# Rows of 260 columns instead of 272 for the fp32r activations of a two-block transformer kernel

## What is computed

```
h = concat(meta_tokens, x)                                   # 272 tokens
proj = rmsnorm(h, norm1_w) @ w_in                            # q k v r glr pu
h = h + concat(o_gla, o_pool) @ w_out                        # mixed heads
h = h + square(relu(rmsnorm(h, norm2_w) @ mlp_w1)) @ mlp_w2  # inner width 8192
x = rmsnorm(h, final_norm_w)[16:]                            # 256 tokens
x = layer_norm(ALPHA * x + hybrid_mixer(x))                  # x @ w_in_2, @ w_out_2
x = layer_norm(ALPHA * x + (mem_attention(x @ w_q)) @ w_o)
x = layer_norm(ALPHA * x + (silu(x @ w_g) * (x @ w_u)) @ w_ffn_out)   # inner width 5632
```

## Time and profile before

| | before |
|---|---|
| median of 3 runs | 2639.5 us |
| lowest, highest | 2638.65, 2639.68 us |
| span of the profiled execution | 2636.7 us |
| mean granted TensorE clock in it | 0.999 |
| TensorE matmuls busy | 2614.3 us (99%), 17248 matmuls |
| VectorE busy | 1565.8 us (59%) |
| ScalarE busy | 1196.8 us (45%) |
| HBM | 177 GB/s over the span |

### The profile page before, as it was taken

How to read it: one execution, slowest core, us unless ns; L and a number is a source line. 1 busy time by engine, 2 the same in 40 slices (tenths; PEclk the granted TensorE clock), 3 DMA queues, 4 the chain that set the end, 5 groups by cost and what they waited for, 6 DMA issues and landing times.

```text
span 2636.7 us, 44070 instructions
## 1 busy us (share of the span) xinstructions
PE 2614.3 (99%) x17248; PEld 2386.1 (90%) x17248; DVE 1565.8 (59%) x2115; ACT 1196.8 (45%) x1608; POOL 27.1 (1%) x65
## 2 busy tenths in 40 slices
PE   9999999999999999999999999999999999999998
PEld 7999889889899899898998999988899988888886
DVE  5544755555555555565744556666866677666655
ACT  5543444444444344534444554444544444444442
POOL 1000000000000000000000000000000000000000
PEclk9999999999999999999999999999999999999999
DMA  7564455555555565564434455554477645777653
GB/s 250 176 179 120 172 178 184 185 190 186 195 178 190 191 188 183 170 222 129 146 128 159 151 186 186 181 209 161 138 198 191 181 169 195 189 191 191 191 183 120
DMA packets 467830, 468.81 MB, mean 178 GB/s; under 512 B 9294, under 2 KB 384190, under 8 KB 466910
## 3 DMA queue, kind: packets, MB, share of 16 engines
q1 hardware_dynamic: 465648, 459.31, 56.0%
q0 software_dynamic: 2064, 7.82, 0.8%
HBM read 464.93 MB, written 2.10 MB: 177 GB/s over the span
## 4 chain that ended last, share of the span: by engine, by line
PE 94%; DVE 3%; ACT 1%; DMA 1%; issue 0%; SPq 0%; DVEq 0%; ACTq 0%
PE ps L662 16%; PE ps L664 16%; PE ps L663 16%; PE ps L692 11%; PE ps L693 11%; PE ps L691 11%; PE ps L659 6%; PE ps L660 3%; DMA raw<-in_w_kv_mem 1%; DVE w_lo L2005 1%; PE ps L1069 1%; PE ps L1122 1%; PE ps L1128 1%; PE ps L752 0%; PE ps L1093 0%
## 5 line engine op out<-in xcount | busy, mean ns | idle before, releaser
L2005 DVE TENSOR_TENSOR w_lo<-raw,w_hi 128x1024 fp32r<-128x1024 f32 (+1 forms) x876 | 1053.2, 1210 | 843.7 <-ACT w_hi L1375 841.5
L1375 ACT ACTIVATE w_hi<-raw 128x1024 fp32r<-128x1024 f32 (+1 forms) x876 | 908.5, 1046 | 975.2 <-PE ps L664 475.7
L662 PE MATMUL ps<-xa,w_hi 128*128 128x256 f32 (+2 forms) x3328 | 951.1, 286 | 1.4 <-DVE w_lo L2005 1.4
L664 PE MATMUL ps<-xa,w_lo 128*128 128x256 f32 (+2 forms) x3328 | 941.0, 283 | 0.0
L663 PE MATMUL ps<-xa,w_hi 128*128 128x256 f32 (+2 forms) x3328 | 936.3, 281 | 0.0
L662 PEld LDWEIGHTS ps<-xa,w_hi 128*128 128x128 f32 x3328 | 627.6, 189 | 12.2 <-issue 9.5
L663 PEld LDWEIGHTS ps<-xa,w_hi 128*128 128x128 f32 x3328 | 629.3, 189 | 1.5 <-issue 0.5
L664 PEld LDWEIGHTS ps<-xa,w_lo 128*128 128x128 f32 x3328 | 627.8, 189 | 0.0
L659 PE MATMUL ps<-xa,w_hi 128*128 128x512 f32 x704 | 246.4, 394 | 0.0
L693 PE MATMUL ps<-w_hi,xh 128*128 128x512 f32 x512 | 201.2, 393 | 0.0
L692 PE MATMUL ps<-w_lo,xh 128*128 128x512 f32 x512 | 201.0, 392 | 0.0
(11 more groups left out here) (349 smaller groups left out, 2562.4 us busy)
## 6 DMA issues: line engine op xcount, KB each, us to landing
raw<-in_mlp_w SPq DMA_DIRECT2D x128, 1024.0 KB
raw<-in_w_in SPq DMA_DIRECT2D x106, 1024.0 KB
raw<-in_w_ffn_in SPq DMA_DIRECT2D x176, 512.0 KB
raw<-in_w_ffn_out SPq DMA_DIRECT2D x40, 1024.0 KB
raw<-in_w_out SPq DMA_DIRECT2D x32, 1024.0 KB
raw<-in_w_o_dsa SPq DMA_DIRECT2D x8, 1024.0 KB
raw<-in_w_o_moba SPq DMA_DIRECT2D x8, 1024.0 KB
raw<-in_w_kv_mem SPq DMA_DIRECT2D x7, 1024.0 KB
```

The source lines that it names most:

```text
L662: nc.tensor.matmul(o, hi, x_hi, start=opens and ci == 0, stop=False)
L664: ins = nc.tensor.matmul(o, lo, x_hi, start=False, stop=closes and ci == 3)
L1375: return nc.scalar.activation(dst, src, ACT.Copy, **kw)
L2005: V.tensor_tensor(w_lo[:, ps_ % CUT, 0:n], raw[:, bs % RAW, n * half:n * half + n], w_hi[:, ps_ % CUT, 0:n].bitcast(F32), ALU.subtract).th ...
```

## The change

The buffers that hold 256 or 258 tokens get rows of `ROW` = 260 columns (1040 bytes). `xa` keeps its size; two views are laid over it: `xt` with rows of 272 for the first block's input, which has 272 tokens, and `xa` with rows of 260 for all later contents. `xh`, `xm` and `xf` get rows of 260. The SwiGLU's `xf` is now shorter, so the memory attention's heads move from chunk 16 to chunk 17 (to stay behind `xd`, which lies over the same bytes), and `qx` starts 64 columns further on (to stay behind chunk 20 of `xf`). `xb`, `xo`, `xd` and the weights' buffers stay where they are, and `region` and `xa` begin at the same bytes as before. Every engine has the same instructions with the same sizes in the same order and with the same waits.

Residues of the rows' starts, in bytes modulo 512, for chunk c:

| buffer | hi before | lo before | hi after | lo after |
|---|---|---|---|---|
| `xa` | 128c | 128c + 64 | 32c | 32c + 16 |
| `xh`, `xm`, `xf` | 128 + 128c | 192 + 128c | 128 + 32c | 144 + 32c |

```diff
@@
+ROW = SEQ + 4
...
-        xa = sb("xa", [P, DC, 2, TOK], F32R)
+        x_rows = sb("xa", [P, DC * 2 * TOK], F32R)
+        xt = x_rows[:].rearrange("p (c a n) -> p c a n", c=DC, a=2)
+        xa = x_rows[:, 0:DC * 2 * ROW].rearrange("p (c a n) -> p c a n", c=DC, a=2)
...
-        xh = over("xh", [P, DC, 2, TOK])
-        xm = over("xm", [P, DC, 2, TOK])
-        xf = over("xf", [P, FF_CH, 2, TOK])
+        xh = over("xh", [P, DC, 2, ROW])
+        xm = over("xm", [P, DC, 2, ROW])
+        xf = over("xf", [P, FF_CH, 2, ROW])
...
-        qx = reg(10880, H_MEM, SEQ)
-        O_MEM = 16
+        qx = reg(10944, H_MEM, SEQ)
+        O_MEM = 17
...
             def from_tokens(c):
-                return xa[:, c, 0, X0:TOK], xa[:, c, 1, X0:TOK]
+                return xt[:, c, 0, X0:TOK], xt[:, c, 1, X0:TOK]
+
+            def from_xt(c):
+                return xt[:, c, 0, :], xt[:, c, 1, :]
...
-            straight(ph["v"], 0, 4, from_xa(TOK), TOK)
+            straight(ph["v"], 0, 4, from_xt, TOK)
...
-                    copy(xa[:, c, 0, :], step_bank(("xT", c))[:, 0:TOK], scale=vec[:, V_N1 + c:V_N1 + c + 1]).then_inc(turned_hi, 1)
+                    copy(xt[:, c, 0, :], step_bank(("xT", c))[:, 0:TOK], scale=vec[:, V_N1 + c:V_N1 + c + 1]).then_inc(turned_hi, 1)
```

More of the change, by code:

```diff
@@ L843, in _ @@
             f = ph["glr"]
-            pair(f.b0, 0, f.t0, 0, from_xa(TOK), TOK, ready=x_chunk, one=True)
+            pair(f.b0, 0, f.t0, 0, from_xt, TOK, ready=x_chunk, one=True)
             def gate_side():
@@ L877, in _ @@
             straight(ph["qk"], 0, 2, from_tokens, SEQ)
-            straight(ph["qk"], 2, 2, from_xa(TOK), TOK)
+            straight(ph["qk"], 2, 2, from_xt, TOK)
             finish()
@@ L945, in _ @@
             side[0] = gla_side()
-            straight(ph["pu"], 0, 4, from_xa(TOK), TOK)
+            straight(ph["pu"], 0, 4, from_xt, TOK)
             finish()
@@ L2153, in tokens_side @@
                     dve.wait_ge(turned_hi, TURNED["xT"] + c + 1)
-                    taken(V.scalar_tensor_tensor(out=xa[:, c, 1, :], in0=step_bank(key)[:, 0:TOK], scalar=vec[:, V_N1 + c:V_N1 + c + 1],
-                                                 in1=xa[:, c, 0, :].bitcast(F32), op0=ALU.mult, op1=ALU.subtract), key)
+                    taken(V.scalar_tensor_tensor(out=xt[:, c, 1, :], in0=step_bank(key)[:, 0:TOK], scalar=vec[:, V_N1 + c:V_N1 + c + 1],
+                                                 in1=xt[:, c, 0, :].bitcast(F32), op0=ALU.mult, op1=ALU.subtract), key)
                     if c % 3 == 2:
```

## The result

| | before | after |
|---|---|---|
| median of 12 runs each, us | 2639.11 | 2643.45 |
| lowest, highest, us | 2637.99, 2639.87 | 2643.2, 2644.8 |
| ratio, 95% interval | | 1.0017, 1.001 to 1.0025 |
| span of the profiled execution, us | 2636.7 | 2643.1 |
| TensorE matmuls busy, us | 2614.3 | 2621.5 |

The change costs 4.3 us, 0.17%: inside the bound of 0.2% that I drew for "no change", though twelve runs a side resolve it as a small loss. The executions of both kernels fall into two groups 1.4 us apart, six and six before and ten and two after, and from the shorter group alone the change costs 5.1 us (2638.35 to 2643.43 in the mean). In the page of the changed kernel TensorE's time is what moved against the earlier trace rows; the other engines' busy times stay within 1 us.

What follows compares the result with a forecast made beforehand. TensorE was taken as bound by its own matmul stream. +0.15 ns on each of 13456 matmuls added 2.0 us to the 2636.7 us span, giving 2638.7; 2.8 us from span to median gave 2641.5 us, range 2614 to 2666.

Steps and rivals of the forecast that it cites:

- The frame: Whole kernel: no instruction, byte, wait or column changes, only matmul spacings; writers of moved rows cost nothing.
- The most likely case: Whole kernel: no change within 0.2% (5.3 us), forecast 2641.5 us, own range 2634 to 2645 us; chance 0.34.
- my nearest rows: `xd` (-0.4 ns a matmul) and `from_tokens` (+0.3 ns), giving a case range of -5.4 to +4.0 us.
- my own sign: Touched stages: forecast wrong if mean spacing moves by over 0.4 ns, or TensorE's waits grow by over 5 us.
- stationary rows, 1216 triples: Products with stationary activations: +0.15 ns a matmul, +0.5 us; upper end `xb`'s pace, +2.3 ns, 8.4 us.
- moving rows of `xa`, 256 columns: 2096 triples on `xa`: +0.15 ns a matmul, +0.9 us; upper end +1.69 ns, the pace of rows of 256.
- 258 columns, 704 triples: 258-column products on `xa`: +0.15 ns a matmul, +0.3 us.
- wide pairs: Wide form, 704 pairs: +0.15 ns a matmul, +0.2 us; upper end 2.8 us, lower end 9.6 us gained.
- The rival of `xb`'s pace: Touched stages: closer hi, lo and chunk residues cost as in `xb`, 25 us slower, 2665 us; chance 0.20.
- Half-filled reads: Lo rows at odd multiples of 16 bytes: 1.56 ns each, 4016 times, +6.3 us, 2645.8 us; chance 0.14.
- The faster rival: Touched matmuls: spread residues remove part of the 6.8 ns independent of columns, 1.5 ns each, -20 us, 2619 us; chance 0.32.
- My test for "it is not the rows": Stages `v`, `pu`, `o`, `kvv` must keep times to a few tenths of a us; otherwise rows aren't the cause.

Runs made afterwards that it cites:

- experiment 5: Rows of 264 in `xa` alone, 272 in `xh`, `xm` and `xf` as in the kernel before; 2632.13 us, ratio 0.9974.
- experiment 3: Rows of 264 instead of the changed kernel's 260 in `xa`, `xh`, `xm` and `xf`; 2638.8 us, ratio 1.0 to the kernel before.
- experiment 11: Rows of 256 in `xa` (all at residue 0) and `xh` (all at 128), SwiGLU's first product reading rows of 272; 2652.43 us, one run.
- experiment 12: Experiment 6 with `xh`, `xm`, `xf` and `out2`'s rows set to 256 columns, stationary rows there at residue 0; 2617.39 us, ratio 0.9917 to the kernel before.
- experiment 10: Experiment 5's rows with all distances kept, `xa` beginning 32 bytes later and `xh` 16 bytes later, weights unmoved; 2638.75 us, one run.
- experiment 1: Changed kernel with `xa` back at rows of 272, rows of 260 only in `xh`, `xm` and `xf`; 2643.42 us, ratio 1.0017 to the kernel before.
- experiments 6: Experiment 5 with three views of `xa`: rows of 264 for 256-column products, 272 for `out2`, 268 for SwiGLU's first product; 2627.59 us, ratio 0.9957.
- experiment 9: Experiment 5's rows with all distances kept, `xa` beginning 16 bytes later and `xh` 32 bytes later, weights unmoved; 2636.53 us, one run.

## Why the prediction was right, and where it was not

**The frame held.** But for the clock's 1.4 us nothing but the spacing of TensorE's matmuls changed, no wait grew, and the writers of the moved rows cost nothing. 2643.45 us lies in the range and in the case's own range of 2634 to 2645 us, 2 us above the forecast. The most likely case, within 0.2%, came true, on its slow side.

**There was luck in it.** The forecast was +2.0 us; the change costs 4.3 us by the medians and 5.0 us between the profiled executions without the clock's part, just inside the 5.3 us that I called no change, and above the +4.0 us that my nearest rows allowed. The chances of the three signs (0.34, 0.34, 0.32) were nearly even, so the case was hardly told apart. By my own sign I was wrong: I had said so for a mean spacing in the touched stages that moves by over 0.4 ns, and it moved by 6.2 us / 13456 = 0.46 ns. Also, the 2.8 us that I put between span and median came from the median of three runs and the span of one; in a profiled execution the time is 1.7 us above its own span (2644.8 and 2643.1 us in the changed kernel).

**The sum was right partly because terms cancelled.** I had spread +0.15 ns over all 13456 matmuls. The profiled executions show instead:

| term | forecast, us | measured, us |
|---|---|---|
| stationary rows, 1216 triples | +0.5 | +6.1 |
| moving rows of `xa`, 256 columns | +0.9 | 0.0 |
| 258 columns, 704 triples | +0.3 | -0.8 |
| wide pairs | +0.2 | +0.9 |
| stage `o`, rows untouched | 0 | -1.0 |

The measured ones are the change of the mean triple times the number of triples: for `xh` 512 x 5.1 ns, for `xm` 128 x 5.6, for `xa` 64 x 5.2 and 128 x 6.6, for `xf` 176 x 3.4 and 176 x 5.6; the 32 triples of `om`, all near side steps, are left out. The 0.0 of the moving rows is a sum too: -0.4 us in MLP up, +0.4 in the second block's input products. The step that failed is the value for stationary rows. I took it from `xd` and `from_tokens`, which are both moving rows; the only stationary neighbour was `xb`, at +2.3 ns a matmul, and +1.6 ns came. By the rule of taking the nearest row of the same kind, this term alone should have stood near its upper end. And the -0.4 ns of `xd` was read from the stage's first 24 matmuls, before it had settled: behind the second side step of the same stage its triples repeat 361, 371, 364, 364 ns, 365.0 in the mean, which is 0.9 ns a matmul above `xa`. It looks like the two paces of experiment 5, seen in the kernel before.

**The rival of `xb`'s pace** had the right size for its stationary part and a wrong mechanism. Rows of 264 are farther apart than of 260 and dearer (experiment 3), and rows that all coincide are among the dearest or the cheapest according to where they coincide (11, 12). **Half-filled reads** are refuted by experiments 3 and 10. **The faster rival** did not come with 260, but its ground, that the part which doesn't grow with the columns can be had, is real: rows of 264 take 1.6 ns from each matmul of MLP up and the residue 0 takes 3.3 ns from each stationary one.

**My test for "it is not the rows" was wrong.** I wrote that an untouched stage that moved would acquit the rows. Stage `o` moved by 1.0 us because the rows of `xa`, which are read in the stage ahead of it, changed: 360 ns a triple with rows of 272 there (the kernel before, experiment 1), 356 ns in all twelve other kernels. In stage `o` `xa` is also written, so the writes could have been it; but in experiments 6 and 11 rows of 272 are written there, only the stage ahead reads others, and the pace is 356 ns. That it is what came before, and not `o` itself, is shown as far as one profiled execution of each kernel can show it; what state is handed on is open. The spacing can also turn within a stage (experiment 5), so one trace need not stand for all executions.

The rule that I weighed, of the Trainium skill's page "TensorE: Matmul & The Clock Gate", Part 2, that the moving operand and the weight load come through independent read ports, is a statement on ports. Taken to mean that a row's place is free it doesn't agree with these traces: experiments 9, 10 and 12 show that the place costs or saves 1 to 3 ns a matmul. Why is open. I did not try to move the weights' buffers, which alone could tell a place against the weights from a place in the memory, nor moving rows at residues between those shown, nor a stage with no weight loads beside it.

## What to carry to other kernels

Where TensorE never waits, read the spacing of matmuls by stage, from a count over a stretch, before looking for anything else: a per cent can lie in where the operands begin. Try the row distance and start of each operand by stage, moving and stationary apart, because one setting for all can cancel itself (experiment 3). Don't carry a price from moving to stationary rows, and expect that a stage's pace may depend on the stage ahead of it. Read a pace from a settled stretch, and see whether the profiled execution's time is that of the others before you carry its numbers on.

## What the runs showed of the hardware

- With 512 moving columns in float32r the spacing went from 226.7 ns (680.1 a triple, experiment 12) to 232.4 ns (697.3, experiment 3) with the stationary rows' place; with 256 moving columns from 116.7 ns (350.1) (experiments 3 and 5) to 120.0 ns (360.0, experiment 11) with the moving rows' place. A shift of 16 bytes with all distances kept moved the first by 1.0 ns (experiment 10) and the second by 1.1 ns (experiment 9).
- In the steady part of a stage the times of the triples repeat. In MLP down they do so after as many chunks as bring a row back to the same residue modulo 256 bytes with rows of 272 (2 chunks, the kernel before), 264 (4, experiment 3) and 260 (8, the changed kernel). It is no general rule: the shifted rows of 272 repeat after 1 chunk (experiments 9 and 10), and rows that all begin at residue 128 after 7 triples (experiment 11).
- Equal instructions with operands at equal addresses ran at two paces: 356 and 360 ns a triple in stage `o`, 361.7 and 365.0 ns in the 258-column product of experiment 3, both in one execution. After an interruption a stage can take a few matmuls to settle (experiment 11).
